# Split rows of the tokens stored by feature row, ahead of a gather on TensorE

## What is computed

```python
h = layer_norm(DEEPNORM_ALPHA * h + mix, ln1_g, ln1_b)      # 256 x 1024 (and 16 meta rows)
group_probs = softmax(t @ router_group_w + router_group_b)  # 4 groups
exp_logits = einsum("td,gde->tge", t, router_expert_w) + router_expert_b
...                                                          # best group, its two best experts
hid = silu(einsum("td,edf->tef", t, expert_w_gate[gi])) * einsum("td,edf->tef", t, expert_w_up[gi])
hid = hid * combine[:, gi, :, None]
y = y + einsum("tef,efd->td", hid, expert_w_down[gi])
```

## Time and profile before

| | |
|---|---|
| median of 3 runs | 827.79 us (827.59 to 828.42) |
| profiled execution | 826.47 us, of which 824.6 us is the span from first to last instruction |
| TensorE busy | 768.2 us, 93% of the span |
| VectorE busy | 484.2 us, 59% |
| ScalarE busy | 373.7 us, 45% |
| moved from HBM | 191.83 MB read, 234 GB/s over the span |
| chain that ended last | TensorE 71%, DMA 17%, VectorE 6% |

### The profile page before, as it was taken

How to read it: one execution, slowest core, us unless ns; L and a number is a source line. 1 busy time by engine, 2 the same in 40 slices (tenths; PEclk the granted TensorE clock), 3 DMA queues, 4 the chain that set the end, 5 groups by cost and what they waited for, 6 DMA issues and landing times.

```text
span 824.6 us, 16208 instructions
## 1 busy us (share of the span) xinstructions
PE 768.2 (93%) x6678; PEld 645.2 (78%) x6678; DVE 484.2 (59%) x838; ACT 373.7 (45%) x568; POOL 54.8 (7%) x94
## 2 busy tenths in 40 slices
PE   8999999999999999999999999999999977677675
PEld 6999998999999998999998999899954533344342
DVE  4555667767676678867854355387774533323325
ACT  4555764554544556567454554474331211111113
POOL 2200041000000000110101000000000000000000
PEclk9999999999999999999999999999999989879889
DMA  9954362655556554544352233449989999999993
GB/s 309 301 194 138 118 178 91 203 173 183 194 166 200 192 169 151 176 132 153 103 155 67 91 103 103 152 155 372 421 330 422 420 419 421 420 422 420 422 419 145
DMA packets 89027, 193.82 MB, mean 235 GB/s; under 512 B 3630, under 2 KB 69521, under 8 KB 76546
## 3 DMA queue, kind: packets, MB, share of 16 engines
q1 hardware_dynamic: 86640, 186.66, 61.8%
q0 software_dynamic: 1888, 4.61, 1.8%
q10 hardware_dynamic: 434, 1.62, 0.5%
HBM read 191.83 MB, written 1.05 MB: 234 GB/s over the span
## 4 chain that ended last, share of the span: by engine, by line
PE 71%; DMA 17%; DVE 6%; ACT 2%; issue 1%; SPq 1%; DVEq 0%; ACTq 0%
DMA expert_w<-in_expert_w_up 16%; PE PG L2026 15%; PE PG L2028 14%; PE PG L2027 14%; PE PG L2635 3%; PE PM L2026 3%; PE PM L2028 3%; PE PM L2027 3%; PE PM L2486 1%; ACT whi L851 1%; SPq L677 1%; PE PM L2665 1%; DMA raw<-in_moba_w_qkv 1%; PE PG L2657 1%; PE PM L2111 1%
## 5 line engine op out<-in xcount | busy, mean ns | idle before, releaser
L2026 PE MATMUL PG<-hT_hi,whi 128*128 128x256 f32 (+1 forms) x816 | 235.5, 289 | 1.1 <-DVE hT_lo L1372 1.1
L2028 PE MATMUL PG<-hT_hi,wlo 128*128 128x256 f32 (+1 forms) x816 | 230.5, 282 | 0.0
L2027 PE MATMUL PG<-hT_lo,whi 128*128 128x256 f32 (+1 forms) x816 | 230.4, 282 | 0.0
L1354 DVE TENSOR_TENSOR wlo<-raw,whi 128x2048 fp32r<-128x2048 f32 x73 | 167.2, 2291 | 66.7 <-ACT whi L851 66.5
L2026 PEld LDWEIGHTS PG<-hT_hi,whi 128*128 128x128 f32 x816 | 153.9, 189 | 7.3 <-issue 4.1
L2028 PEld LDWEIGHTS PG<-hT_hi,wlo 128*128 128x128 f32 x816 | 154.1, 189 | 0.0
L2027 PEld LDWEIGHTS PG<-hT_lo,whi 128*128 128x128 f32 x816 | 153.5, 188 | 0.2
L851 ACT ACTIVATE whi<-raw 128x2048 fp32r<-128x2048 f32 x73 | 139.4, 1910 | 22.3 <-PE PG L2028 20.0
L2635 PE MATMUL PG<-expert_w,xw 128*32 128x256 f32 x992 | 73.2, 445 | 34.8 <-DMA expert_w<-in_expert_w_up 34.8
L2635 PEld LDWEIGHTS PG<-expert_w,xw 128*32 128x32 f32 x992 | 35.9, 124 | 57.3 <-issue 45.3
L1939 DVE SCALAR_TENSOR_TENSOR y_lo<-PG,small,y_hi 128x512 fp32r<-128x512 f32 x16 | 12.0, 750 | 94.1 <-ACT y_hi L1281 94.1
(11 more groups left out here) (525 smaller groups left out, 1334.5 us busy)
## 6 DMA issues: line engine op xcount, KB each, us to landing
expert_w<-in_expert_w_gate SPq DMA_DIRECT2D x32, 1024.0 KB, 26.7
expert_w<-in_expert_w_up SPq DMA_DIRECT2D x32, 1024.0 KB, 26.5
expert_w<-in_expert_w_down SPq DMA_DIRECT2D x32, 1024.0 KB, 26.8
raw<-in_ffn_w_up SPq DMA_DIRECT2D x22, 1024.0 KB, 5.1
raw<-in_w_in SPq DMA_DIRECT2D x22, 1024.0 KB, 5.3
raw<-in_moba_w_qkv SPq DMA_DIRECT2D x12, 1024.0 KB, 5.5
raw<-in_ffn_w_down SPq DMA_DIRECT2D x11, 1024.0 KB, 4.9
raw<-in_moba_w_o SPq DMA_DIRECT2D x4, 1024.0 KB, 5.3
```

What stands on the lines that cost most here:

```text
L1354: dve.tensor_tensor(lo_of(n), raw[:, n % R, :], hi_of(n).bitcast(F32), ALU.subtract).then_inc(s_lo, 1)
L2026: pe.matmul(dst, lh, rh, start=start, stop=False, **kw)
L2027: pe.matmul(dst, lh, rl, start=False, stop=False, **kw)
L2028: return pe.matmul(dst, ll, rh, start=False, stop=stop, **kw)
```

## The change

`X_hi` and `X_lo` are stored with the eight feature rows one behind the other, 128 words each, instead of in the order of `X`. The two instructions that write them keep their number, size and place in the program; they now read `X` through a view that steps by 8 words (`by_feature`) and write 1024 words in a row (`rows_lo` also reads `X_hi` in a row). The 32 weight loads of the gather read 128 neighbouring words. Semaphores, waits, buffers and transfers stay as they are.

```diff
-        X_hi = [place(f"X_hi{t}", [P, D], at, F32R) for t, at in enumerate((63232, 33536))]
-        X_lo = [place(f"X_lo{t}", [P, D], at, F32R) for t, at in enumerate((67328, 29440))]
+        X_hi = [place(f"X_hi{t}", [P, KD, P], at, F32R) for t, at in enumerate((63232, 33536))]
+        X_lo = [place(f"X_lo{t}", [P, KD, P], at, F32R) for t, at in enumerate((67328, 29440))]
+
+        def by_feature(t):
+
+            return X[:, t, :].rearrange("p (n k) -> p k n", k=KD)
+
...
-                act.activation(X_hi[t][:, :], X[:, t, :], ACT.Copy).then_inc(s_xhi3, 1)
+                act.activation(X_hi[t][:, :, :], by_feature(t), ACT.Copy).then_inc(s_xhi3, 1)
...
-                dve.tensor_tensor(X_lo[t][:, :], X[:, t, :], X_hi[t][:, :].bitcast(F32), ALU.subtract).then_inc(s_xlo, 1)
+                dve.tensor_tensor(X_lo[t][:, :, :], by_feature(t), X_hi[t][:, :, :].bitcast(F32), ALU.subtract).then_inc(s_xlo, 1)
...
-                    mine = (X_hi, X_lo)[i][t][:, :].rearrange("p (n k) -> p k n", k=KD)[:, k, :]
+                    mine = (X_hi, X_lo)[i][t][:, k, :]
```

## The result

The changed kernel takes **832.11 us** (median of five runs, 831.78 to 834.3), the kernel before 827.59 (826.6 to 828.42) beside it: a ratio of 1.0061, interval 1.005 to 1.0072. By the medians it is slower by 4.5 us, by the ratio 5.0 (4.1 to 6.0), where 2.3 were forecast. The profiled execution took 832.11 us, its span 830.4.

A forecast was written before the change was run, and what follows sets the result against it. The expert-weight stream, which starts when the gather ends, was taken to bound the kernel. 1.75 us at the first tile + 0.89 at the second X_lo - 0.30 on TensorE gave +2.34 us, 830.1 us, range 827.9 to 832.2.

The forecast's parts named there:

- The chain of cause: From about 606 us a fixed volume of expert weights streams; moving the gather's end moves the kernel's end one for one.
- a: Extra time of each ScalarE X_hi copy, 1024 elements, for reading X in steps of 8 words: 1.11 us.
- d: Extra time of each VectorE X_lo subtraction, 1024 elements, for reading X in steps of 8 words: 0.89 us.
- 1.91: Price in ns per hopping read, from the gather's weight-load spacing, 245/128 ns a column, taken for both engines.
- 1.75 forecast: Delay in us at the second tile's column, 586.34: a + d less the 0.25 us gap on VectorE.
- 0.30: Saving in us on TensorE by contiguous weight loads in the gather's last twelve matmuls, 0.18 to 0.41.
- the sum of 2.34: Delay in us at the issue behind the gather, 604.39, and at the end: 1.75 + 0.89 - 0.30.
- From there every step hangs on VectorE: From the second tile's column at 586.34 to the second X_lo at 594.74, the delay stays 1.75 us.
- heavy hops: Rival: hopping reads cost 2.58 ns an element on both engines, 4.38 us in sum, 832.2 us; chance 0.13.
- Free hops: Rival: both engines read X as fast as before, only TensorE's 0.30 us saving remains, 827.5 us; chance 0.14.
- one engine: Rival: hopping reads slow only VectorE (1.23 us, 829.0) or only ScalarE (0.56 us, 828.4); chance 0.18.
- a change that doesn't do what it says: Rival: the gather's 245 ns spacing isn't from the hop, TensorE saves nothing, sum 2.64 us, 830.4 us; chance 0.07.

The follow-up runs named there:

- experiment eight: Kernel before with small stepped reads and writes added at its end on VectorE and ScalarE; steps of 8 words cost 0.78 and 1.02 ns an element more.
- experiment five: Changed kernel plus six dummy products ahead of the wait for the second tile's last column and five ahead of feature row 5; 829.99 us, ratio 1.0029.
- Experiment one: Changed kernel plus six dummy products on TensorE while it waits for the second tile's last column; 829.92 us, ratio 1.0029.
- two: Kernel before plus two contiguous subtractions on VectorE ahead of the first X_lo, layout unchanged; 831.39 us, ratio 1.0051.
- nine: Changed kernel without the nine dummy products ahead of the second tile's rank products; 830.22 us, ratio 1.0028.
- experiment ten: Kernel before without the nine dummy products ahead of the second tile's rank products; 828.17 us, ratio 1.0005.
- experiment six: Kernel before with both X_lo subtractions moved from VectorE to GpSimd, old layout; 829.81 us, ratio 1.003.
- experiment three: Kernel before with the new layout for the second token tile alone; 828.41 us, ratio 1.001.
- experiment seven: Changed kernel with both X_lo subtractions moved from VectorE to GpSimd, new layout; 830.28 us, ratio 1.0042.

## Why the prediction missed

**Right.** The chain of cause: the stream of expert weights starts when the gather ends. From the issue to the end of the span are 220.2 us before and 221.0 after. The prices: a = 1.05 against 1.11 and d = 0.99 and 0.84 against 0.89. That the spacing of the hopping weight loads gave these prices is luck in part. By the same reading contiguous loads cost 227/128 = 1.77 ns a column, where the two engines read contiguously at 1.05 and 0.83 ns; so most of the spacing is something other than the price of a read. That 1.91 lies near the 1.83 and 1.85 ns an element that experiment eight gives (1.05 + 0.78 and 0.83 + 1.02) is not shown to have one cause. The difference of the two records, (330 - 188)/128 = 1.11 ns a column, would have given 1.14 us for a and for d. The second X_hi costs nothing (592.21 + 2.12 lies 4.85 before the X_lo that wants it). The column of the second tile is late by 1.82 (1.75 forecast). TensorE's loads became contiguous: the group of the 32 weight loads after has 188 ns as its median, the last eleven intervals of the gather (605.42 to 608.09) have a mean of 243 ns with the first and 232 without it (245 before, 227 forecast), and the saving is 4.84 - 4.58 = 0.26, against 0.30. With the clock held (experiment five) the remaining difference is 2.2 us against the sum of 2.34.

**Wrong.** One step of the sum, the one that reads "From there every step hangs on VectorE (column, statistics, router of tile 1, ranks, pick), and TensorE and ScalarE wait for it, so 1.75 us arrive at 594.74". It shifts the whole stretch rigidly. At 594.74 arrived 1.82 + 2.14 = 3.96 us. The step took TensorE to be the same after its wait as before it. But TensorE had 1.59 us of idle time where it had none before, its clock fell by half, and its dummies, which had ended with the marks at full clock, ended 2 us after them (the marks were written by 593.2, the products that want them began at 595.25). Experiment one takes the 2.14 away without touching the change, two makes the loss without the change, nine takes the dummies away, and 1.9 of the wait is gone even at the low clock. The profile of before did hold the warning: nine dummy products just ahead of the ranks say that something there needs TensorE busy.

**The rivals.** The heavy hops gave 832.2 and the measurement 832.11, but that is chance: they want 1.79 and 1.57 us for a and d, and the table has 1.05 and 0.9. Free hops, one engine, and a change that doesn't do what it says are refuted by the same rows. The range held the median by 0.09 us, because its upper end was taken for the heavy hops (the mean of the five runs, 832.54, lies above it); no case in it was about the clock.

**What stays open.** The two profiled executions differ by 5.64 us, the medians by 4.5. Of the 5.64 the stage explains 4.58 and the lateness at 582 0.45; the rest, 0.6, lies in the stream (418 against 420 GB/s). The kernel before varies as well: of nineteen executions beside experiments nine and ten, twelve had a mean granted clock of 0.969 and took 826.90 to 828.79 us, seven had 0.971 to 0.974 and took 826.55 to 827.75. The one trace of an execution of the first kind does not differ in the stage of the change. Experiment eight is the kernel before up to its last results, and its one run has a mean clock of 0.969 (827.50 us). There, too, the clock is 1.00 from 580 to 606 us, and the issue comes at 604.48:

```profile
604.48 0.33 SPq L679 DMA_DIRECT2D expert_w<-in_expert_w_up  x1
```

But its output transfers begin 214.8 us after the issue, at 819.28, where the kernel before has 214.0 (818.39). So about 0.8 us of the scatter lies in the stream, where the clock falls now and again in the kernel before too (0.89 in the mean from 606 to 800). What sets these 0.8 us is not shown. Nor is why the medians of experiment ten show so little of its 1.41 us. A part of it is the choice of executions: the profiled one of the kernel before, at 826.47, is below all nineteen, and that of experiment ten, at 828.15, is at the median of its ten. And it stays open what makes the clock fall: a wait of 0.38 us for the column was followed by it in experiment six, waits of 1.09 and 1.32 us elsewhere in experiments three and seven were not. None of the kernels tried was faster than the kernel before.

## What to carry to other kernels

A delay that makes TensorE wait can cost it half its clock, and then more than the delay itself (here after waits of 0.38 to 2.08 us, though not after every one): when you shift a stretch, ask of each engine that waits what it does after the wait, and read the granted clock there. Dummy work that keeps TensorE busy helped here where it stood in the wait; queued ahead of work that another engine needs, it takes nearly twice as long when the clock is gone (4.19 us in place of 2.25). And a layout that spares hops on TensorE, where loads overlap (245 - 232 = 13 ns each here), should not move them to engines on which every element pays (1.0 and 0.8 to 1.0 ns).

## What the runs showed of the hardware

- Reading float32 in steps of 2 words cost nothing on VectorE and ScalarE, 4 words and more 0.78 to 0.97 ns an element on VectorE and 1.0 on ScalarE; a second stepping source on VectorE cost no more (0.62 us either way). A destination stepping by 2 words was free (0.43 us), by 4 it cost as much as a source (0.61).
- After 1.59 us without work TensorE's granted clock went from 1.00 to 0.50; after 1.24 us in experiment one and 0.38 us in experiment six, likewise. After 1.09 us in experiment three and 1.32 us in experiment seven it stayed at 1.00, and in experiment five, with dummies in both waits, as well.
- A VectorE operation with both sources in SBUF stood still while GpSimd subtracted (2.23 us in place of 0.19).
